# Norms made in transposed form, modulation rows as columns, gates broadcast by DMA, output projections stream by stream

## The reference

```python
for l in range(2):
    mc, ms = ada_mod(c_ctx, mod_w[l], mod_b[l]), ada_mod(c, mod_w[l], mod_b[l])   # 6 rows of 1024 each
    h = rms_norm(x, norm1_g[l]) * (1.0 + m[1]) + m[0]      # for each stream, with its own m
    o = even_mixer(h) if l == 0 else odd_mixer(h)          # HGRN2 and attention, or retention
    x = x + m[2] * (o @ w_out)
    h = rms_norm(x, norm2_g[l]) * (1.0 + m[4]) + m[3]
    x = x + m[5] * hier_moe(h)      # 32 experts: best group of 8 of 4 groups, in it the best two experts
y = rms_norm(x, final_norm_g)
```

## Time and profile before

| | us |
|---|---|
| median of 3 runs | 1103.02 |
| the profiled execution | 1103.07 |
| its span, first to last instruction | 1100.9 |
| PE busy | 959.7 (87%) |
| DVE busy | 300.6 (27%) |
| ACT busy | 193.7 (18%) |
| HBM read and written | 316.34 and 6.03 MB |

### The profile page before, as it was taken

One profiled execution on the slowest core, in us unless ns is written; L12 is line 12 of the kernel. 1 busy time (PEld: TensorE's weight loads), 2 busy tenths in 40 slices (PEclk: granted clock), 3 DMA queues, 4 the chain that ended last, 5 costly groups with the idle time before them and its releaser, 6 DMA issues.

```text
span 1100.9 us, 13296 instructions
## 1 busy us (share of the span) xinstructions
PE 959.7 (87%) x5597; PEld 514.6 (47%) x5597; DVE 300.6 (27%) x656; ACT 193.7 (18%) x350; POOL 24.8 (2%) x45
## 2 busy tenths in 40 slices
PE   3899999798999977967799999999997999868863
PEld 0475445544665544533344444444444665445431
DVE  1323347704531211100414122231016312111103
ACT  1111114402210100000220222443012110000001
POOL 2000000000000000000000011000000000000000
PEclk9999999998999998987899999999997999989987
DMA  9999969970399999999954343047420799999992
GB/s 292 398 394 403 340 263 396 414 306 12 113 363 418 418 418 415 420 416 400 389 190 153 133 177 147 2 172 285 149 99 1 300 365 415 417 418 415 416 417 85
DMA packets 77793, 323.27 MB, mean 294 GB/s; under 512 B 4892, under 2 KB 4948, under 8 KB 61092
## 3 DMA queue, kind: packets, MB, share of 16 engines
q1 hardware_dynamic: 74756, 312.78, 72.0%
q0 software_dynamic: 2976, 9.61, 2.4%
HBM read 316.34 MB, written 6.03 MB: 293 GB/s over the span
## 4 chain that ended last, share of the span: by engine, by line
PE 61%; DMA 22%; SPq 8%; DVE 5%; ACT 2%; issue 2%; DVEq 0%
PE PS L593 59%; DMA ring<-in_moe_w_down 15%; SPq L500 7%; DMA ring<-in_moe_w_gate 5%; DMA ring<-in_mod_w 2%; DVE H L1497 1%; DVE scratch L1487 1%; PE PS L639 1%; SPq L467 0%; ACT L1174 0%; DVE scratch L1522 0%; DVE X L1524 0%; ACT scratch L1172 0%; PE PS L1112 0%; SPq L486 0%
## 5 line engine op out<-in xcount | busy, mean ns | idle before, releaser
L593 PE MATMUL PS<-ring,scratch 128*32 128x256 f32 (+4 forms) x2720 | 309.1, 469 | 71.4 <-DMA ring<-in_moe_w_gate 34.2
L593 PE MATMUL PS<-ring,HT 128*128 128x512 f32 x576 | 254.1, 598 | 3.8 <-issue 2.7
L593 PEld LDWEIGHTS PS<-ring,scratch 128*32 128x32 f32 (+2 forms) x2720 | 149.6, 129 | 228.5 <-issue 191.8
L593 PEld LDWEIGHTS PS<-ring,HT 128*128 128x128 f32 x576 | 109.0, 192 | 137.4 <-issue 135.3
L593 PE MATMUL PS<-scratch 128*128 128x512 f32 (+2 forms) x440 | 117.0, 437 | 4.4 <-issue 1.5
L1935 DVE TENSOR_TENSOR scratch<-PS,scratch 128x256 f32<-128x256 f32 x20 | 8.5, 425 | 283.9 <-ACT scratch L1328 283.9
L593 PEld LDWEIGHTS PS<-scratch 128*128 128x128 f32 (+1 forms) x440 | 56.1, 193 | 59.8 <-issue 55.6
L593 PE MATMUL PS<-scratch,H 128*128 128x128 f32 x640 | 81.1, 282 | 0.0
L593 PEld LDWEIGHTS PS<-scratch,H 128*128 128x128 f32 x640 | 75.9, 195 | 9.2 <-issue 9.2
L593 PE MATMUL PS<-ring,cpad 128*32 128x512 f32 x384 | 47.5, 632 | 13.0 <-DMA ring<-in_mod_w 12.9
L1328 ACT ACTIVATE scratch<-PS 128x256 f32<-128x256 f32 x20 | 7.7, 383 | 263.1 <-PE PS L593 263.1
(11 more groups left out here) (273 smaller groups left out, 616.4 us busy)
## 6 DMA issues: line engine op xcount, KB each, us to landing
ring<-in_moe_w_gate SPq DMA_DIRECT2D x56, 1024.0 KB, 18.6
ring<-in_moe_w_up SPq DMA_DIRECT2D x56, 1024.0 KB, 21.8
ring<-in_moe_w_down SPq DMA_DIRECT2D x56, 1024.0 KB, 22.9
ring<-in_mod_w SPq DMA_DIRECT2D x24, 2048.0 KB, 13.8
ring<-in_odd_w_in SPq DMA_DIRECT2D x12, 2048.0 KB, 19.7
ring<-in_even_w_in SPq DMA_DIRECT2D x7, 2048.0 KB, 21.1
ring<-in_moe_w_gate SPq DMA_DIRECT2D x4, 2048.0 KB, 15.9
ring<-in_moe_w_up SPq DMA_DIRECT2D x4, 2048.0 KB, 18.1
```

The costliest lines, as they stand in the source:

```text
L593: return nc.tensor.matmul(out, lhsT, rhs, start=start, stop=stop, skip_group_check=True, **kw)
```

## The change: what it does

- **Norm.** `spread` (ACT) squares half a row at a time; DVE makes a diagonal matrix with the inverse roots (`diagonal`), and PE multiplies `X`, every eighth column as the stationary operand, with it (`turn`). That gives the normed tokens already transposed. ACT and DVE copy it out in pieces of 128x128 with a scale and a shift of one number for each partition (`evac_ht`). For the MoE, `H` comes from transposing `HT` back (`turn_back`, `evac_h`).
- **Modulation rows.** A `mod_w` block is laid out in four groups of 256 columns in place of two halves by two parities, so that DVE's 32x32 transpose gives columns (`turn_rows`, `gain_cols`, `shift_cols`). All matmuls that broadcast a row are gone, and the calls of `keep_warm` and `start_zero`. The gates go from `modrow` to DRAM and back by a DMA that copies them to all partitions (`rows`, `gate_rows`, on POOL).
- **Projections.** Stream 0 is projected whole, then stream 1 half by half, so residual, norm and logits of stream 0 run beside stream 1's matmuls. In the even layer the first half of stream 0 stands before the attention of stream 1; in the odd layer the transposes of the gated values stand between the chunks.
- **Router.** Logits come with tokens on partitions; the choice is made for each stream apart, in 16 DVE operations (`choose`); the weights (`weights`) are computed behind `who`.
- **Start.** Four bias transfers in place of eight, no gain, 0.5 MB less of constants, one more weight item ahead of the other constants; POOL's router weights and small parameters wait for the second `mod_w` block.
- **Ends of MoE.** The scatter and the residual go stream by stream, the residual by halves.

```diff
             for l in range(2):
-                mb = A["mod_b"][l].rearrange("(b h n) -> h b n", h=2, n=BANK)
-                for half in range(2):
-                    for s in range(S):
-                        r = 32 * half + 2 * l + s
-                        sp.dma_start(modrow[r:r + 1, :, :], mb[half:half + 1]).then_inc(bias_in, 16)
+                mb = A["mod_b"][l].rearrange("(b q n) -> q b n", q=4, n=ROW)
+                for s in range(S):
+                    sp.dma_start(modrow[2 * l + s::32, :, :], mb).then_inc(bias_in, 16)
             sp.dma_start(X[:, 0, :], A["x_prompt"][0]).then_inc(x_in, 16)
             sp.dma_start(X[:, 1, :], A["x_sample"][0]).then_inc(x_in, 16)
-            sp.dma_start(gain[:, :], A["norm1_g"][0].partition_broadcast(P)).then_inc(first_gain_in, 16)
             load(2)
             load(3)
+            load(4)
             sp.wait_ge(params_in, 64)
             sp.dma_start(const[:, NFIRST:], A["consts"][:, NFIRST:]).then_inc(params_in, 16)
-            n = 4
+            n = 5
...
+            for l in range(2):
+                for i, name in enumerate(("norm1_g", "norm2_g")):
+                    pool.dma_start(gcol[:, l, i, :], A[name][l].rearrange("(p k) -> p k", k=KT)).then_inc(gcol_in, 16)
...
+                pool.wait_ge(mod_ready, 3 + MOD_LATE.index((l, b)))
+                for s in range(S):
+                    pool.dma_start(mod_rows[l, b // 3, s].rearrange("(q n) -> q n", q=4), modrow[2 * l + s::32, b, :])\
+                        .then_inc(rows_out[l][b // 3], 16)
+
+            pool.wait_ge(mod_ready, 2)
...
+            def gate_rows(dst, l, i, signal):
+                pool.wait_ge(rows_out[l][i], 16 * S)
+                pool.dma_start(dst[:, :, :].rearrange("p s n -> p (s n)"),
+                               mod_rows[l, i].rearrange("s n -> (s n)").partition_broadcast(P)).then_inc(signal, 16)
+
+            pool.wait_ge(group_done, 4)
+            pool.wait_ge(state_out, 32)
+            gate_rows(GATE1, 0, 0, gate1_in)
...
-                        for half in range(2):
-                            g = 2 * (k % 2) + half
-                            mm = matmul(PS[32 * g:32 * g + 32, bank, :], cpad[:, 4 * q + k, 2 - 2 * l:34 - 2 * l],
-                                        w[:, k, BANK * half:BANK * half + BANK],
-                                        start=(q == 0 and k < 2), stop=(q == 1 and k >= 2))
+                        for g in range(4):
+                            mm = matmul(PS[32 * g:32 * g + 32, bank, 0:ROW], cpad[:, 4 * q + k, 2 - 2 * l:34 - 2 * l],
+                                        w[:, k, ROW * g:ROW * g + ROW], q == 0 and k == 0, q == 1 and k == 3)
...
+            def turn(n, s, bank):
+
+                pe.wait_ge(diag_ready, 2 * n + s + 1)
                 for k in range(KT):
-                    mm = nc.tensor.transpose(PS[:, 2 * s + k // 4, P * (k % 4):P * (k % 4) + P],
-                                             H[:, s, k, :], ident)
+                    mm = matmul(PS[:, bank + k // 4, P * (k % 4):P * (k % 4) + P], X[:, s, k::KT], DIAG[:, s, :], True, True)
                 mm.then_inc(ht_done, 1)
...
+            def project(kind, src, s, half, kks, last):
+
+                for kk in kks:
+                    item = (kind, kk // 4)
...
                     w = ring[:, slot(item), :].rearrange("p (k n) -> p k n", k=4)
-                    for k in range(4):
-                        kk = 4 * q + k
-                        for s in range(S):
-                            for half in range(2):
-                                mm = matmul(PS[:, 2 * s + half, :], src[:, kk, P * s:P * s + P],
-                                            w[:, k, BANK * half:BANK * half + BANK],
-                                            kk == 0, kk == 4 * chunks - 1)
-                    mm.then_inc(used, 1)
-                pe.wait_ge(scale_ready, 4 * l + 4)
-                shifts(n + 1, l, 3)
-                turn_h(n + 1)
-
+                    mm = matmul(PS[:, 2 * s + half, :], src[:, kk, P * s:P * s + P],
+                                w[:, kk % 4, BANK * half:BANK * half + BANK], kk == 0, kk == last)
+                    if s == 1 and half == 1 and kk % 4 == 3 and kk < last:
+                        mm.then_inc(used, 1)
+                return mm
...
+            def project_second(kind, src, l, last):
+
+                n = 2 * l + 1
+                project(kind, src, 1, 0, range(last + 1), last).then_inc(out_done, 1)
+                turn(n, 0, 4)
+                project(kind, src, 1, 1, range(2), last)
+                turned(n, 0)
+                logits(l, 0)
+                project(kind, src, 1, 1, range(2, last + 1), last).then_inc(used, 1)
+                turn_back(0)
+                turn(n, 1, 6)
+                turned(n, 1)
+                logits(l, 1)
+                turn_back(1)
+
+            turn_probs(0)
+            attend(0)
+            pe.wait_ge(mix_ready, 3)
+            for half in range(2):
+                project("even_out", HT, 0, half, range(4), KT - 1)
+            turn_probs(1)
+            attend(1)
+            for half in range(2):
+                mm = project("even_out", HT, 0, half, range(4, KT), KT - 1)
+            mm.then_inc(out_done, 1)
...
+            def spread(n, s):
+
+                for half in range(2):
...
+                    A_(squares[:, half, :], X[:, s, BANK * half:BANK * half + BANK], SQUARE,
+                       accum_out=sumsq[:, 2 * s + half:2 * s + half + 1]).then_inc(sums_ready, 1)
+                    act.wait_ge(sums_ready, 4 * n + 2 * s + half + 1)
+                    if half == 0:
+                        A_(rest[:, s:s + 1], sumsq[:, 2 * s:2 * s + 1], IDENTITY, scale=1.0 / D, bias=EPS_COL)\
+                            .then_inc(rest_ready, 1)
+                act.wait_ge(rest_ready, 2 * n + s + 1)
+                std = sumsq[:, 2 * s + 1:2 * s + 2]
+                A_(std, std, SQRT, scale=1.0 / D, bias=rest[:, s:s + 1]).then_inc(std_ready, 1)
...
+                    A_(HT[:, k, P * s:P * s + P], PS[:, bank, P * k:P * k + P], IDENTITY,
+                       scale=cols[:, l, i, 1, s, k:k + 1], bias=cols[:, l, i, 0, s, k:k + 1]).then_inc(ht_ready_a, 1)
...
+            def turn_norm(l):
+
+                n = 2 * l + 1
+                spread(n, 0)
+                evac_ht(n, 0)
+                spread(n, 1)
+                evac_h(l, 0)
+                evac_ht(n, 1)
+                evac_h(l, 1)
...
+            def diagonal(n, s):
 
                 dve.wait_ge(std_ready, 2 * n + s + 1)
...
-                    V.tensor_copy(HT[:, 4:8, P * s:P * s + P], PS[:, 2 * s + 1, :].rearrange("p (k t) -> p k t", k=4))\
+                st.link(V.reciprocal(rstd[:, s:s + 1], sumsq[:, 2 * s + 1:2 * s + 2]))
+                V.tensor_scalar(DIAG[:, s, :], ident, rstd[:, s:s + 1], None, ALU.mult).then_inc(diag_ready, 1)
...
+            def residual(n, s, half):
+
+                gate, part = (GATE2 if n % 2 else GATE1), slice(BANK * half, BANK * half + BANK)
+                st.link(V.tensor_tensor(gate[:, s, part], PS[:, 2 * s + half, :], gate[:, s, part], ALU.mult))
+                V.tensor_tensor(X[:, s, part], X[:, s, part], gate[:, s, part], ALU.add).then_inc(x_ready, 1)
...
+                def first(values, best, ties, hot):
+
+                    st.link(V.tensor_reduce(best, values, AX, ALU.max))
+                    st.link(V.scalar_tensor_tensor(out=hot, in0=values, scalar=best, in1=cst(ties),
+                                                   op0=ALU.is_ge, op1=ALU.mult))
+                    st.link(V.tensor_reduce(tie, hot, AX, ALU.max))
+
+                first(lg4, top[:, 0:1], "tie4", g4)
+                st.link(V.tensor_scalar(g4, g4, tie, -1.0, ALU.is_equal, ALU.add))
+                st.link(V.scalar_tensor_tensor(out=e32.rearrange("p (g e) -> p g e", g=NG),
+                                               in0=bcast(g4.unsqueeze(2), [P, NG, EG]), scalar=BIG,
+                                               in1=lge.rearrange("p (g e) -> p g e", g=NG), op0=ALU.mult, op1=ALU.add))
+                first(e32, top[:, 1:2], "tie32", HOT1[:, s, :])
+                st.link(V.tensor_scalar(HOT1[:, s, :], HOT1[:, s, :], tie, None, ALU.is_equal))
+                st.link(V.scalar_tensor_tensor(out=e32, in0=HOT1[:, s, :], scalar=-BIG, in1=e32,
+                                               op0=ALU.mult, op1=ALU.add))
+                first(e32, top[:, 2:3], "tie32", HOT2[:, s, :])
+                st.link(V.tensor_scalar(HOT2[:, s, :], HOT2[:, s, :], tie, None, ALU.is_equal))
+                V.tensor_tensor(MASK[:, s, :], HOT1[:, s, :], HOT2[:, s, :], ALU.add).then_inc(mask_ready, 1)
...
+            def enter_moe(l):
+
+                n = 2 * l
+                dve.wait_ge(out_done, 2 * l + 1)
+                dve.wait_ge(gate1_in, 16 * (l + 1))
+                residual(n, 0, 0)
+                residual(n, 0, 1)
+                diagonal(n + 1, 0)
```

(64 more changed lines are left out.)

598 lines of the change are left out of this document (244 added, 354 removed).

## The result

The changed kernel takes 1065.95 us (median of 4 runs, 1064.8 to 1068.17), the kernel before 1103.59 beside it: a ratio of 0.9659, 95% interval 0.9645 to 0.9674. The forecast of 1049 had the sign right and is 17 us too fast; the places are those that it named, and the two MoEs, where it expected nothing. The time lies in the stated range, but outside the likeliest case's own (1038 to 1063) and near the rival *half lost on the new chains* (1070).

What follows compares the result with a forecast made beforehand. PE was taken to bound the even and odd layers and the weight stream the MoEs; cuts in five chains, 13.0 + 16.4 + 4.9 + 18.4 + 1.7 = 54.4 us, gave 1048.7, say 1049, from about 1103; range 1036 to 1074.

Steps and rivals of the forecast that it cites:

- half lost on the new chains: Rival: turns at the upper price (7 us) and a cold PE (12 to 16) lose some 20 us: 1070; chance 0.22.
- Start: Up to the first even matmul: 13.0 us gained, at 36.4 instead of 49.59.
- I put the last item at 29: Start: the last of four weight items lands at 29 us instead of 36.5.
- The terms behind the items: Start: second block done at 32.4, row sum and transpose 1.0, copies 2.3; first even matmul put at 36.4.
- I take the lower end, because the loads run on their own: Turns: a strided load of X costs as a transpose does, 0.25 us each, 1.9 for a turn of eight.
- The upper bound: Turns: strided loads at 1.5 times, from DVE's permuted shift: 0.9 us more for a turn, 7 for eight.
- Entrances: Ways into the MoEs, to their first tiles: 16.4 us gained at MoE 0 and 18.4 at MoE 1.
- I give it against a cold clock: Entrance of MoE 0: some 2 us of removed zeroing set off against PE's cold clock.
- The order of DVE's last work: Entrance, stream 1's chain: selection 0.5, ranks to `who` 5.2, weights 1.9, weighing and copy 1.2 us.
- the rival whose ends don't move: Rival: the stream sets the MoE ends by bytes alone, both entrances (34.8 us) are given back: 1084; chance 0.05.
- End: After stream 0's last scatter: residual halves, square, root, inverse and product end at 1096.1 for 1097.8, 1.7 us gained.
- The slower rival: Strided load of X at eight times makes a turn 15.2 us: 1155; break-even 6.8 more per turn; chance 0.04.

Runs made afterwards that it cites:

- experiment 7: Changed kernel plus contiguous turn operand, fillers at MoE entrances, DVE's copy before the weights, and fillers ahead of the first turn and behind MoE 0: 1048.09 us, ratio 0.9488.
- experiment 6: Changed kernel with router weights, norms, biases and decay fetched at once, not behind the second modulation block: 1069.15 us, ratio 0.9682.
- experiment 1: Changed kernel with X kept feature-chunk by feature-chunk, so a turn's stationary operand is contiguous, with strided residual additions on DVE: 1056.38 us, ratio 0.9568.
- experiment 2: Changed kernel with twenty-four 128x128 filler matmuls on constants in four of TensorE's waits at each MoE entrance: 1062.54 us, ratio 0.9628.
- experiment 5: Changed kernel with fillers at MoE entrances, and DVE copying tile 0's gathered tokens before computing the weights: 1057.81 us, ratio 0.9581.
- experiment 3: Changed kernel with four one-row, 512-column matmuls that zero the sums' banks put back into tile 0 of each MoE: 1080.87 us, ratio 0.9776.

## Why the prediction came out as it did

**Start: 4.1 short.** The step "I put the last item at 29" was off by 2.3 (31.3 in experiment 7), but did not show: the two turns held PE until 32.16, since they took 7.92 and not 3.8. Of what was to bring the items forward, only the hold on the router weights has an experiment, and it is worth 1.7 (experiment 6). The terms behind the items add to 35.7 and not to the 36.4 that the forecast goes on with; from the second block's end (35.8) to the first even matmul it took 4.9, where they have 3.3.

**Turns.** The failed step is "I take the lower end, because the loads run on their own". PEld's busy time of the earlier trace rows is that of contiguous operands, and it said nothing of a strided one, where a load and its matmul take 0.24 and PEld is busy all through. The upper bound, 1.5 times from DVE's shift, was too low as well: it is twice, 3.84 for 1.95. For eight turns that is some 16 us over the forecast, the shortfall's size; experiment 1 gave back 9.6, as low clocks and DVE's strided additions kept the rest. "Wrong if a turn takes over 3 us" was the forecast's own sign, and it came. The Trainium skill (SBUF — State Buffer, "Door 1: The DMA port swizzle") had the sign: beyond four fp32 a step costs. The trace agrees at full clock, 3.84 against 1.95 at a step of eight. It should have weighed more than a row of another engine.

**Entrances: 7.7 and 6.2 short.** Of MoE 0's 7.7, 1.8 are the first turn and 2.3 the second; logits cold 2.0, prefix sums 0.9, the choice 0.8, the rest small and of both signs. "I give it against a cold clock", 2 us of zeroing for the whole clock, was the second step that failed: experiment 2 got back 2.6 and 1.5 at the two entrances by the clock alone, until DVE bound, and some 2 more at each once DVE's copy no longer stood in the way (experiment 5). *Half lost* had this clock at 12 to 16 and the turns at 7. The experiments gave back 8.1 by fillers and copy together and 9.6 by the turns: its sum was near, its parts were not.

**The order of DVE's last work** was right: selection, ranks, weights and copy 8.4 against 8.8. But I did not see that the copy stood behind the weights for no reason (experiment 5).

**MoE ends.** They move with tile 0, as said, more exactly with the end of its up projection (experiment 3); the rival whose ends don't move is refuted. That the zeroing had stood in tile 0, on this very path, I counted under the entrance and not under the MoE: 1.5 us at each, unforecast. Both MoEs together gave 4.0 that no term had. Without them the time would be 1070, that of *half lost*: that the forecast comes out as near as it does is in part luck.

**End** and the way of the gates came out. Stream 0's residual waited for its sums, not for its gate. The end's 1.7 for 1.7 is in part luck: its terms add to 1095.6 and not to 1096.1, and the 0.5 stands where the table load of stream 0's root, which has no term, delays stream 1's last square on ACT by 0.6. The slower rival would have needed turns of 8.7 us; they took 3.8 to 4.2.

## What to carry to other kernels

Price a matmul by its stationary operand's layout too: here a step of 32 bytes doubled the turn at full clock, and cost little where the clock was at half. When fillers and broadcasts go, look at what they kept warm: the serial stretch behind was paid here at a clock of 0.60, and once that was mended the next engine's order showed. A stream-bound stretch still begins with one chain: here, a microsecond up to the end of the first tile's up projection was about a microsecond at the MoE's end.

## What the runs showed of the hardware

- With a 128x128 fp32 stationary operand at a step of 32 bytes, a load and its matmul take 0.24 us in a run of them at full clock, with a contiguous one 0.12 (3.84 and 1.95 for 16 records). The strided turn hardly changes with the granted clock, 3.84 at 1.00, 4.09 at 0.61 and at 0.58; a contiguous one does, 1.95 at 1.00, 2.62 at 0.76 and 3.79 at 0.50.
- Being busy did not keep the clock: 4.28 us of matmuls with a single row, without a gap that a row shows, and the granted clock fell from 1.00 (2.4 GHz) to 0.50 (1.2 GHz) for 6.5 us, most of it in the next projection. At MoE 1 it was 0.68 in the 5 us behind 3.77 us of them.
